# Zeroed products ahead of the first ones, FFN products round the turn behind the per-layer gate, and an output chunk ahead of MoBA's last pair: three edits to a transformer kernel

## The reference, cut to what matters

```python
# first block
rq, rk, rv, rg, mq, mk, mv, ga, gb = split(rmsnorm(x) @ w_in)
a = (silu(rg) * retention(rot(rq), rot(rk), rv)) @ w_ret_out
b = moba_attention(norm(mq), norm(mk), mv) @ w_moba_out    # 8 heads of 64, softmax over 256 keys
x = x + (sigmoid(ga) * a + sigmoid(gb) * b) @ w_o
x = x + (silu(h @ w_gate) * (h @ w_up)) @ w_down           # h = rmsnorm(x)
# second block, end of layer 0 and start of layer 1
gate = sigmoid(x @ ple_w_gate + ple_b_gate)
x = layer_norm(ALPHA * x + gate * (p @ ple_w_proj))        # "site 5"
kv = x @ kv_w_down                                          # keys and values of layer 1
x = layer_norm(ALPHA * x + 0.5 * swiglu(x, ffn_in, ffn_out))
```

## Time and profile before

| | before |
|---|---|
| median of 3 runs | 1500.08 us |
| lowest and highest | 1499.92 and 1500.76 us |
| the profiled execution | 1500.31 us |
| its span, first to last instruction | 1498.2 us |
| PE busy in the span | 1477.7 us (99%) |
| PE weight loads (PEld) | 1275.1 us (85%) |
| DVE, ACT, POOL busy | 928.7, 793.2, 190.1 us |
| HBM to SBUF and back | 183 GB/s over the span |

### The profile page before, as it was taken

How to read it: one execution, slowest core, us unless ns; L and a number is a source line. 1 busy time by engine, 2 the same in 40 slices (tenths; PEclk the granted TensorE clock), 3 DMA queues, 4 the chain that set the end, 5 groups by cost and what they waited for, 6 DMA issues and landing times.

```text
span 1498.2 us, 21332 instructions
## 1 busy us (share of the span) xinstructions
PE 1477.7 (99%) x8040; PEld 1275.1 (85%) x8040; DVE 928.7 (62%) x1207; ACT 793.2 (53%) x975; POOL 190.1 (13%) x56
## 2 busy tenths in 40 slices
PE   8999999999999999999999999999999999999997
PEld 6888788888888888888888888888888998888886
DVE  7476455666656665525766668765666565766667
ACT  6436545444444445666544456644446664544456
POOL 0015211000040000372100001000005441100010
PEclk9999999999999999999999999999999999999999
DMA  9545456666546555552565557565555336555562
GB/s 345 185 142 177 135 177 198 217 195 196 186 159 214 184 186 177 187 170 85 196 222 183 186 194 228 176 223 184 186 192 164 124 113 197 196 197 188 184 216 71
DMA packets 187545, 274.73 MB, mean 183 GB/s; under 512 B 10048, under 2 KB 137184, under 8 KB 187488
## 3 DMA queue, kind: packets, MB, share of 16 engines
q1 hardware_dynamic: 183568, 262.77, 53.3%
q10 hardware_dynamic: 3920, 11.18, 2.3%
HBM read 272.83 MB, written 1.05 MB: 183 GB/s over the span
## 4 chain that ended last, share of the span: by engine, by line
PE 91%; DVE 5%; ACT 2%; issue 1%; DMA 0%; DVEq 0%; SPq 0%; ACTq 0%
PE bank L720 23%; PE bank L727 12%; PE acc L584 7%; PE acc L583 7%; PE acc L582 7%; PE bank L582 6%; PE bank L584 6%; PE bank L583 6%; PE bank L766 3%; PE acc L893 2%; PE acc L578 2%; PE bank L629 2%; PE bank L636 2%; PE bank L644 2%; DVE w_lo L1859 1%; PE bank L951 1%
## 5 line engine op out<-in xcount | busy, mean ns | idle before, releaser
L1859 DVE TENSOR_TENSOR w_lo<-w_raw,w_hi 128x2048 fp32r<-128x2048 f32 (+1 forms) x208 | 472.9, 2278 | 165.6 <-ACT w_hi L1410 121.3
L720 PE MATMUL bank<-xT,w_hi 128*128 128x512 f32 x1520 | 361.3, 390 | 0.0
L507 POOL TENSOR_TENSOR w_lo<-w_raw,w_hi 128x2048 fp32r<-128x2048 f32 (+1 forms) x41 | 176.9, 4321 | 1264.9 <-ACT w_hi L1326 1264.9
L720 PEld LDWEIGHTS bank<-xT,w_hi 128*128 128x128 f32 x1520 | 282.6, 188 | 56.6
L1410 ACT ACTIVATE w_hi<-w_raw 128x2048 fp32r<-128x2048 f32 x145 | 276.4, 1906 | 0.0
L1326 ACT ACTIVATE w_hi<-w_raw 128x2048 fp32r<-128x2048 f32 (+4 forms) x105 | 189.4, 1817 | 29.1 <-PE bank L584 10.1
L727 PEld LDWEIGHTS bank<-xT,w_lo 128*128 128x128 f32 x1520 | 189.3, 192 | 3.9
L727 PE MATMUL bank<-xT,w_lo 128*128 128x256 f32 x1520 | 191.4, 284 | 0.0
L582 PE MATMUL acc<-w_hi,sTh 128*128 128x512 f32 x400 | 155.9, 390 | 0.0
L583 PE MATMUL acc<-w_lo,sTh 128*128 128x512 f32 x400 | 155.9, 390 | 0.0
L584 PE MATMUL acc<-w_hi,sTl 128*128 128x512 f32 x400 | 155.8, 390 | 0.0
(11 more groups left out here) (231 smaller groups left out, 2030.0 us busy)
## 6 DMA issues: line engine op xcount, KB each, us to landing
w_raw<-in_ffn_w_in SPq DMA_DIRECT2D x176, 512.0 KB, 4.4
w_raw<-in_ffn_w_out SPq DMA_DIRECT2D x88, 512.0 KB, 4.2
w_raw<-in_w_in SPq DMA_DIRECT2D x52, 512.0 KB, 4.8
w_raw<-in_fox_w_in SPq DMA_DIRECT2D x24, 512.0 KB, 4.6
w_raw<-in_w_ffn_gate SPq DMA_DIRECT2D x22, 512.0 KB, 4.7
w_raw<-in_w_ffn_up SPq DMA_DIRECT2D x22, 512.0 KB, 4.5
w_raw<-in_w_ffn_down SPq DMA_DIRECT2D x22, 512.0 KB, 4.2
w_raw<-in_ple_w_gate SPq DMA_DIRECT2D x16, 512.0 KB, 4.5
```

Source lines behind the costliest of these rows:

```text
L507: pool.tensor_tensor(w_lo[s][:, 0:cols], w_raw[u % RING][:, 0:cols], w_hi[s][:, 0:cols].bitcast(F32), ALU.subtract).then_inc(w_lo_done[u % ...
L720: mm = pe.matmul(bank[b + m], wh[:, k, m], both, start=k == 0 and not narrow_first, stop=k == KD - 1 and narrow_first, skip_group_check=na ...
L1859: nc.vector.tensor_tensor(w_lo[s][:, 0:cols], w_raw[u % RING][:, 0:cols], w_hi[s][:, 0:cols].bitcast(F32), ALU.subtract).then_inc(w_lo_don ...
```

## The change

Three edits, independent of one another.

1. POOL first clears 256 columns of `tanh`, and PE, ahead of `entry()`, makes six fp32 products of these zeros into a PSUM bank that is not yet used.
2. The PLE site of layer 0. On PE the last six products of g1 go behind the turn of token tile 0 at site 5, and the first products of the FFN's first two units for tile 0 are split so that those of the first unit stand ahead of the turn of tile 1 and those of the second right behind it. On ACT the square-root table is loaded ahead of the sum of squares, `ptanh(0, 1)` goes behind the root, and the FFN's first unit is converted ahead of `ptanh(1, 1)`. On DVE `ple_add(0, 1)` and the low parts of tile 0 move to fit.
3. The chunk ret_out0 becomes the last `fill` item of step 8, so that it stands ahead of the last pair of heads. Only PE's program is changed for this.

```diff
             ENG["pool"] = pool
+            pool.memset(tanh[:, 0, 0:S], 0.0).then_inc(idle_set, 1)
             pool.memset(eps[:, 0:1], LN_EPS).then_inc(eps_set, 1)
...
                 if kv_down:
                     kv_down.run(1, tiles=(0,), phase=1)
-                    to_xT(site, x, tiles=(1,))
                     take(2, ("ffn_out", f, 0))
                     first_of(0, 0, 0)
+                    to_xT(site, x, tiles=(1,))
+                    first_of(1, 0, 0, joins=True)
                     kv_down.run(0, 1, tiles=(1,))
                     first_of(0, 0, 1)
+                    first_of(1, 0, 1, joins=True)
                     take(3, ("ffn_out", f, 0))
                     first_of(0, 1)
-                    first_of(1, 0)
                     first_of(1, 1)
...
+            pe.wait_ge(idle_set, 1)
+            for _ in range(6):
+                pe.matmul(bank[7][:, 0:S], tanh[:, 0, 0:P], tanh[:, 0, 0:S], start=True, stop=True)
             entry()
...
-                       6: [lambda: to_xT("ret", ro, (1,), b0=2)], 7: [gb1[0]]}, {8: [gb1[1]]})
-            need_xT("ret")
-            chunk("ret_out0", (2, 3), slot0=8)
+                       6: [lambda: to_xT("ret", ro, (1,), b0=2)], 7: [gb1[0]],
+                       8: [lambda: need_xT("ret"), lambda: chunk("ret_out0", (2, 3), slot0=8)]}, {8: [gb1[1]]})
...
                 if l == 0:
-                    g1.run(0, 1, tiles=(1,))
+                    g1.run(0, tiles=(1,))
+                    g1.run(1, tiles=(1,), part=0)
+                    to_xT(5, x, tiles=(0,))
+                    g1.run(1, tiles=(1,), part=1)
...
-                if l == 0:
-                    squares_sum(site + 1, 0, False)
-                    ptanh(0, 1)
                 act.wait_ge(act_done, counts["act_done"])
                 root_table()
+                squares_sum(site + 1, 0, False)
+                root(site + 1, 0, False)
...
                 tanh_table()
                 if l == 0:
-                    xT_evac(5, (0,), tiles=(0,))
+                    ptanh(0, 1)
+                    split_to(u0 + 7)
+                    xT_evac(5, tiles=(0,))
+                    split_to(u0 + 8)
                     ptanh(1, 1)
-                    xT_evac(5, (1,), tiles=(0,))
...
                     if t and l == 0:
+                        ple_add(0, 1)
                         split_to(u0 + 7)
-                        xT_evac(5, (0,), tiles=(0,))
+                        xT_evac(5, tiles=(0,))
```

More of the change, by code:

```diff
@@ L352, in build @@
         zeros_set, rope_q_loaded = sem("zeros_set"), sem("rope_q_loaded")
-        gates_placed = sem("gates_placed")
+        gates_placed, idle_set = sem("gates_placed"), sem("idle_set")
         tanh_done = sem("tanh_done")
@@ L768, in first, with first_of @@
                     return mm
-                def first_of(b, t, parts=None):
+                def first_of(b, t, parts=None, joins=False):
                     u, at = u0 + b, (up_slot > gate_slot) == b
@@ L777, in first_of @@
                         need("pe", "xTh", site, t, k // 4)
-                        pe.matmul(out, xTh[:, k, tok], wh[:, k], start=k == 0, stop=False)
+                        pe.matmul(out, xTh[:, k, tok], wh[:, k], start=k == 0 and not joins, stop=False,
+                                  skip_group_check=t == 0)
                     for k in range(KD) if parts != 1 else ():
                         need("pe", "xT", site, t, k // 4)
-                        pe.matmul(out, xTl[:, k, tok], wh[:, k], start=False, stop=False)
+                        pe.matmul(out, xTl[:, k, tok], wh[:, k], start=False, stop=False, skip_group_check=t == 0)
                     if parts == 0:
@@ L785, in first_of @@
                     for k in range(KD):
-                        mm = pe.matmul(out, xTh[:, k, tok], wl[:, k], start=False, stop=k == KD - 1)
+                        mm = pe.matmul(out, xTh[:, k, tok], wl[:, k], start=False, stop=k == KD - 1,
+                                       skip_group_check=t == 0)
                     if t == 1:
@@ L1297, in _ @@
                     kv_down = Chunk("kv_down0", (4, 5), ready=5)
-                    to_xT(5, x, tiles=(0,))
                     kv_down.run(0, tiles=(0,))
@@ L1807, in _ @@
                     last_bias(1, 2)
-                if l == 0:
-                    squares_sum(site + 1, 0, False)
-                    ptanh(0, 1)
                 act.wait_ge(act_done, counts["act_done"])
                 root_table()
+                squares_sum(site + 1, 0, False)
+                root(site + 1, 0, False)
                 if l:
-                    squares_sum(site + 1, 0, False)
-                root(site + 1, 0, False)
-                split_to(u0 + 7)
+                    split_to(u0 + 7)
                 act.wait_ge(act_done, counts["act_done"])
@@ L1936, in mean @@
                         dve.wait_ge(gb_loaded, gb_count(site))
-                    elif site == 5:
-                        rest(0, 1)
-                    elif site not in (4, 8):
+                    elif site not in (4, 5, 8):
                         rest(0, 0)
@@ L2489, in _ @@
                 norm_and_turn(site + 1, finish_ple,
-                              scaled=None if l else lambda: ple_add(0, 1),
                               late=lambda: split_to(u0 + 7), late_too=lambda: split_to(u0 + 8))
```

## The result

The changed kernel takes 1505.84 us (median of 6 runs, 1504.66 to 1507.46), the kernel before 1500.15 in the runs beside it (1499.70 to 1500.76): a ratio of 1.004, 95% interval 1.003 to 1.005. It is slower by 5.7 us. The direction is the one forecast as nearly as likely as no change, and the time lies 0.4 us above the range. The profiled execution took 1505.65 us, its span 1503.4; it is read part by part, in the order of the prediction.

A forecast was written before the change was run, and what follows sets the result against it. TensorE (PE) was taken to bound the kernel, with nine tenths of the chain that ended last. The sum was 1500.3 - 1.6 (zeroed products) - 1.7 (site) + 5.5 (stall) = 1502.5 us, range 1500.8 to 1505.4.

The forecast's parts named there:

- The stall: Between the last MoBA pair and ret_out1: PE stands about 4.6 us for late weights; loss 5.5 us.
- The clock: Behind the long stall: clock falls, ret_out1 starts slowly, costing 2.5 us more (1505.0); a rival outside the sum, chance 0.32.
- The one row: After PE's last work at the kernel's end: the granted clock fell after 3.5 to 3.6 us without work.
- The short stall: At ret_out0's second unit: PE's 0.88 us wait ahead of the pair is saved and waited again there, gain 0.
- The zeroed products: At PE's start: six products of zeros raise the clock early, the third batch starts at 13.1; gain 1.6 us.
- The site: At layer 0's PLE, round the turn of site 5: PE's waits fall from 2.5 to 0.8 us; gain 1.7 us.
- The faster rival: At ret_out1: its weights are converted before the copy and not late, the pair's wait is gone; 1496.1 us, chance 0.07.

The follow-up runs named there:

- the kernel whose clock stays up: The changed kernel with unused products filling both places where PE stands, four in ret_out0's wait and ten between the pair and ret_out1: 1503.09 us.

## Why the prediction was right and wrong

**The stall: right.** The chain of copy, conversion and low part is the one worked out, and the waiting costs 5.6 us by the two runs (the one with both stalls filled and the one without the move), 5.5 in the sum. PE stood 4.7 us where 4.6 was forecast.

**The clock: the step that failed.** "I leave this out of the sum and make it a rival", at 0.32. All six runs are above the 1503.1 of the kernel whose clock stays up, by 1.6 to 4.4 us; what falls cost is part of every run, 2.7 at the median, and the term of 2.5 belonged in the sum. The profiled run's fall is that term: 13 products at 0.43 and not 0.227 are 2.6 us, and it lies 1505.65 - 1503.09 = 2.6 above. The one row was read as a duration that a stall must reach. The runs show no such border: the clock fell behind stalls of 4.7, 3.2 and 2.0 us, the last in some executions only. With the term in the sum the forecast is the rival's 1505.0, inside the range; most of the 0.8 us still missing is the zeroed products, below. The Trainium skill (page "TensorE: Matmul & The Clock Gate") has both sides: the fall 5.2 us after the last matmul in "Seeing it yourself" was no guide here, where it came after 3.2, while its warning in "HAM oscillation", that an idle stretch between bursts puts the clock down, is what the long stall's traces show (it fell at 193.0, 1.5 us before PE's next product).

**The short stall: missed.** "The 0.88 is saved and waited again, gain 0" is right in time. But it put two short waits together into one of 1.96 us, and behind that the clock falls too in some of the runs, by their groups: 5 of 11 with the order changed, 5 of 7 with the long stall filled, 3 of 7 with ACT's order alone changed. The groups lie 1.8, 1.5 and 1.6 us apart. The fall in the long stall alone gives the 1505.7 of the profiled run; the upper end, 1505.4, left no room for the other. The runs at 1507.2 and 1507.5 would fit both falls, and the one at 1504.66 a clock that is down for less of ret_out1, as with ACT's order alone changed; they were not profiled, so this is argued.

**The zeroed products: right in mechanism, too large.** 1.05 us and not 1.6. (The working's 0.85 us a product should be 0.88 by its own row; the six were done at 6.0, so nothing hangs on it.) The sum took the gain against one execution and the earliest start of the third batch. In the profile of the zeroed products alone the batch starts at 13.44 and rv0 at 29.91, 1.15 us ahead of the earlier trace rows; in the changed kernel's 13.11 and 29.58, 1.5 ahead. The rest would follow if the clock rises earlier in other executions of the kernel before than in the profiled one, as the spread of its runs suggests. No profile shows that: in the three that start without zeroed products (before, the site alone, ret_out0 alone) it rises at 12.0 to 12.1 us, and the one with the rise at 10.5 has two zeroed products in front. So it is argued that the products remove a spread rather than a fixed time. The Trainium skill (the same page, section "What's actually happening") says that the cold start varies by run; no two profiles here with the same start bear it out.

**The site: right.** 1.7 us; x of tile 1 came 0.2 us later against PE's arrival than assumed, and 1.0 us of wait is left, not 0.8.

**The faster rival: wrongly priced.** With ret_out1's weights ready it gave 1496.1; the run gave 1498.4 in its faster group. Besides the zeroed products' shortfall it counted the 0.88 as gained, which the prediction's own working says is waited again. The pair had stood in time in which PE would have waited for ret_out0's second unit anyway; moved behind ret_out0 its 0.8 us is on the path. Only with that unit early too does the order win.

With the measured terms: 1500.1 - 1.05 - 1.7 + 5.6 + 2.7 = 1505.7. The last two are differences to the measured time itself, so that the sum closes is no test of them; the 13 products of the profile are one for the clock.

## What to carry to other kernels

When work of the bounding engine is moved ahead of something that another engine waits for, follow that other engine's stream: whatever stands behind its wait, here the next weights' conversion, is late by the whole length of the moved work, unless its order is changed too. Price a stall of TensorE with a fall of its clock behind it, too: here 2.6 us for the one of 4.7 us, and 1.5 to 1.8 in some executions for one of 2.0. Before, with waits of 0.88 and 0.63 us apart from each other, the profile shows no fall, so merging short waits into one is not free. Where one kernel's runs fall into groups, profile one of each before a median is explained.

## What the hardware showed unexpectedly

The clock's fall can come when TensorE is already at work again: 1.0 us after it resumed in one run, 1.5 in another, and the engine then runs 3.4 us at 1.2 GHz. Two idle stretches alike, of 1.96 us in the same place of two kernels, were followed by a fall in one profile and by none in the other. And the granted clock's column says 1.00 for the start of a kernel, before the first recorded rise, while the spacing of products there (0.43 us in the earlier trace rows) shows the lower level. This is the kernel before, six products in 2 us and a granted clock of 1.00:

```profile
8.00:10.00 2.00, 2.00 (x6) 1.53 (x5) 1.73 (x3) 0.87 (x1) 0.00 (x0) 1.00 1.02 398
```
